# Two-layer hybrid decoder: TensorE transposes replaced by VectorE 32x32 transposes and GpSimd transfers

## The chip, the cores and the metric

One core of one Trainium2 chip runs the program. The metric is the device time of one execution in microseconds; lower is better. Times given for the kernel are medians of several executions.

## The reference, cut to what matters

The input is x of 256 tokens by 2048 features in float32. Layer one is stick-breaking attention over 16 heads of 128, layer two softmax attention with rotary embedding. With 256 tokens there is a single 256-position block, so that attention is plain causal attention.

```python
# layer one
q, k, v, z = split(x @ w_in_a, 4)          # w_in_a: 2048 x 8192
y = (stick_breaking(q, k, v) * silu(z)) @ w_out_a
x = layer_norm(alpha * x + y) * g0 + b0
x = x + (p[0] @ w_ple[0]) * sigmoid(x @ w_ple_gate[0])
# shared keys and values, then layer two
xs = layer_norm(x) * g_kv + b_kv
k, v = split(xs @ w_kv, 2); k = rope(k)
q, z = split(x @ w_in_b, 2); q = rope(q)
y = (causal_attention(q, k, v) * silu(z)) @ w_out_b
x = layer_norm(alpha * x + y) * g1 + b1
x = x + (p[1] @ w_ple[1]) * sigmoid(x @ w_ple_gate[1])
```

## The kernel before, in words

Every weight matrix is streamed once in pieces of 256 rows by 512 columns (512 KB), 388 of them and 8 halves at the start. SyncE loads them into four slots of raw. ScalarE copies a piece into w_hi in the reduced format fp32r (`split`, L417), VectorE writes the remainder raw - w_hi into w_lo (`split`, L676), and TensorE makes three products hi*hi, hi*lo, lo*hi for each half of the rows and each of two token tiles, 12 matmuls of 128x512 a piece (`piece`, L1077 to L1079). A chunk is 8 pieces: 512 output columns for all 256 tokens, in two of the four banks of acc, the next chunk in the other two. There are 8 slots of w_hi and w_lo, so the split of piece n + 8 waits until piece n is used, and it is written in the program of ScalarE and of VectorE at the place of piece n.

Around this stream everything else is an inserted step. Each engine's program is written out: in `pieces(n, base, after, before)` (ScalarE, VectorE) and `chunk(..., after)` (TensorE), `after={j: [...]}` means that the step stands behind the split, or the piece, with index j of the chunk. Engines meet through semaphores only.

- Layer one has four groups of 4 heads. Each has a q, k, v and z chunk (the order is q, k, then v, z, q of the next group, k of the next group). `evacuate` (L696) copies the finished chunk to big0, in rows by token. Matmuls of the attention need q, k and z with features on the partitions: `q_turn` behind piece 4 of the k chunk, `k_turn` behind piece 2 of the v chunk and `z_turn` behind piece 2 of the next q chunk transpose them on TensorE, eight 128x128 transposes each, into the PSUM tile aux (`transposes`, L1104; `z_turn`, L1170). ScalarE and VectorE read aux (`q_copies`, `k_copies`, `silu_z`, `queries_lo`, `keys_lo`). `key_scores`, `cumulate` and `weigh_values` are the attention's matmuls.
- The output projection of a layer is followed by one piece for each of four chunks of p @ w_ple (`ple_and_gate`), between which the normed result is transposed for the gate projection (`ln_turn`, L870 applies gain and offset, L430 and L691 split the operand), and by four gate chunks. `sigmoid_gate` and `add_ple` finish a chunk; in layer one `add_ple` leaves the sum in stage, copies it to res (L907), and `x2_turn` transposes it on TensorE for layer two. GpSimd writes the result to x2_spill.
- Layer two has four q chunks, four z chunks and four pairs of key and value chunks. `ln_step` transposes the normed layer-one result (the key/value operand), `q_turn_b` the rotated q, `z_turn_b` z, all on TensorE.
- GpSimd issues only the few transfers of p, tables, residual and spill, and copies q's first half for layer two's attention (L398).

The last gate chunk of layer two ends the stream: two sigmoids, two products, two sums and two stores follow.

## Time and profile before

| quantity | value |
|---|---|
| median of 3 runs | 1170.33 us (1170.27 to 1170.63) |
| the profiled execution's own time | 1170.72 us |
| its span in the profile | 1168.8 us |
| TensorE busy | 1161.9 us, 99% |
| VectorE busy | 740.9 us, 63% |
| ScalarE busy | 591.1 us, 51% |
| GpSimd busy | 21.3 us, 2% |
| moved by DMA | 221.49 MB, mean 189 GB/s |

In the rows, PE is TensorE, PEld its weight load, DVE VectorE, ACT ScalarE, POOL GpSimd and SP SyncE; a q behind the name is that engine's sequencer. L with a number is a line of the kernel. The DMA issues of GpSimd count as busy time of POOL in the timeline.

### The profile page before, as it was taken

To read this page: it belongs to the slowest core of one execution; us is meant where nothing else is said; L and a number is where in the kernel's file an instruction comes from. 1 tells how busy PE (TensorE), PEld (TensorE's weight loads), DVE (VectorE), ACT (ScalarE), POOL (GpSimd) and SP (SyncE) were. 2 spreads that over 40 slices of the span, in tenths; PEclk is the share of its full clock that TensorE was granted. 3 is DMA by queue.
4 is the path that set the end of the run, shared out by engine and by line. 5 is a ranking of instruction groups with operands and counts; after the bars stand their busy time and mean duration, and the time that the engine had idled before them with its cause. 6 is when DMAs were issued, how large, how long until landed. Compare 5 with 4: busy or idle time off the path is not lost.

```text
span 1168.8 us, 15615 instructions
## 1 busy us (share of the span) xinstructions
PE 1161.9 (99%) x5484; PEld 971.4 (83%) x5484; DVE 740.9 (63%) x786; ACT 591.1 (51%) x669; POOL 21.3 (2%) x43
## 2 busy tenths in 40 slices
PE   9999999999999999999999999999999999999998
PEld 7888888888888888888888888888888888888886
DVE  6765556556556556688777665446677666656863
ACT  6665465456446543455444445544555545435541
POOL 1000000000000000000000000000000000000000
PEclk9999999999999999999999999999999999999999
DMA  9855656665565776457765655655545575763671
GB/s 307 287 161 178 181 162 178 179 181 161 165 194 156 241 253 200 137 184 237 232 198 162 197 180 182 193 181 164 169 155 178 167 244 175 252 195 112 211 252 41
DMA packets 112618, 221.49 MB, mean 189 GB/s; under 512 B 6929, under 2 KB 8977, under 8 KB 112065
## 3 DMA queue, kind: packets, MB, share of 16 engines
q1 hardware_dynamic: 110032, 209.74, 57.7%
q0 software_dynamic: 2544, 11.19, 2.7%
q8 instruction: 27, 0.44, 0.1%
q14 instruction: 15, 0.11, 0.0%
HBM read 216.71 MB, written 4.19 MB: 189 GB/s over the span
## 4 chain that ended last, share of the span: by engine, by line
PE 95%; DVE 2%; DMA 1%; ACT 1%; issue 0%; SPq 0%; ACTq 0%; DVEq 0%
PE acc L1077 29%; PE acc L1079 29%; PE acc L1078 29%; PE aux L1104 2%; PE aux L1121 2%; DVE w_lo L676 1%; PE aux L1145 1%; DVE stage L870 1%; PE aux L1159 1%; DMA raw<-in_w_ple_gate 1%; PE aux L1308 0%; DMA raw<-in_w_in_a 0%; DVE act L691 0%; PE aux L1079 0%; PE aux L1078 0%
## 5 line engine op out<-in xcount | busy, mean ns | idle before, releaser
L676 DVE TENSOR_TENSOR w_lo<-raw,w_hi 128x1024 fp32r<-128x1024 f32 x388 | 471.7, 1224 | 358.5 <-ACT w_hi L417 357.2
L417 ACT ACTIVATE w_hi<-raw 128x1024 fp32r<-128x1024 f32 x388 | 409.7, 1060 | 471.3 <-PE acc L1079 424.5
L1077 PE MATMUL acc<-w_hi,act 128*128 128x512 f32 x1552 | 611.9, 394 | 0.2 <-DVE w_lo L767 0.2
L1079 PE MATMUL acc<-w_hi,act 128*128 128x512 f32 x1552 | 605.1, 390 | 0.0
L1078 PE MATMUL acc<-w_lo,act 128*128 128x512 f32 x1552 | 604.1, 389 | 0.0
L1079 PEld LDWEIGHTS acc<-w_hi,act 128*128 128x128 f32 x1552 | 291.3, 188 | 61.8
L1077 PEld LDWEIGHTS acc<-w_hi,act 128*128 128x128 f32 x1552 | 291.5, 188 | 58.6 <-issue 1.0
L1078 PEld LDWEIGHTS acc<-w_lo,act 128*128 128x128 f32 x1552 | 291.7, 188 | 58.1
L430 ACT ACTIVATE act<-stage 128x1024 fp32r<-128x1024 f32 (+1 forms) x12 | 12.7, 1061 | 33.8 <-DVE stage L870 33.8
L513 ACT ACTIVATE heads<-aux,neg_max 128x128 f32<-128x128 f32 (+1 forms) x32 | 13.0, 419 | 23.7 <-DVE neg_max L1000 23.7
L691 DVE TENSOR_TENSOR act<-stage,act 128x1024 fp32r<-128x1024 f32 (+1 forms) x12 | 14.7, 1226 | 14.3 <-ACT act L430 14.3
L870 DVE TENSOR_SCALAR stage<-aux,ln_col 128x256 f32<-128x256 f32 x48 | 22.8, 538 | 0.9 <-PE aux L1104 0.9
L1104 PEld LDWEIGHTS aux<-ident,big 128*128 128x128 f32 x128 | 14.9, 140 | 2.1
L1104 PE MATMUL aux<-ident,big 128*128 128x128 f32 x128 | 16.6, 272 | 0.0
L696 DVE TENSOR_SCALAR big<-acc 128x1024 f32<-128x1024 f32 x12 | 14.6, 1218 | 0.0
L701 DVE SCALAR_TENSOR_TENSOR heads<-aux,heads 128x768 f32<-128x768 f32 x8 | 7.6, 954 | 10.8 <-ACT heads L483 10.8
L430 ACT ACTIVATE act<-heads 128x1024 f32 (+1 forms) x8 | 8.5, 1062 | 10.4 <-DVE heads L752 10.0
L691 DVE TENSOR_TENSOR act<-heads,act 128x1024 f32 (+1 forms) x8 | 9.8, 1225 | 5.7 <-ACT act L430 5.2
L417 ACT ACT_TABLE_LOAD x9 | 11.5, 1283 | 0.2
L630 ACT ACTIVATE stage<-acc 128x512 f32<-128x512 f32 x2 | 1.2, 598 | 19.1 <-PE acc L1079 19.1
L891 DVE TENSOR_TENSOR big<-big,heads (+1 forms) x8 | 9.8, 1225 | 0.9
L943 DVE TENSOR_TENSOR stage<-stage,big 128x512 f32<-128x512 f32 x2 | 1.4, 688 | 14.0 <-ACT stage L630 14.0
(148 smaller groups left out, 617.5 us busy)
## 6 DMA issues: line engine op xcount, KB each, us to landing
raw<-in_w_in_a SPq DMA_DIRECT2D x124, 512.0 KB, 3.7
raw<-in_w_ple_gate SPq DMA_DIRECT2D x64, 512.0 KB, 4.8
raw<-in_w_in_b SPq DMA_DIRECT2D x64, 512.0 KB, 3.7
raw<-in_w_kv SPq DMA_DIRECT2D x64, 512.0 KB, 3.7
raw<-in_w_out_a SPq DMA_DIRECT2D x32, 512.0 KB, 4.4
raw<-in_w_out_b SPq DMA_DIRECT2D x32, 512.0 KB, 4.9
heads<-in_ln_rows POOLq DMA_DIRECT2D x4, 1024.0 KB, 8.2
raw<-in_w_ple SPq DMA_DIRECT2D x8, 512.0 KB, 4.6
```

The costliest lines, as they stand in the source:

```text
L417: nc.scalar.activation(w_hi[:, r], raw[:, r % RAWS], ACT.Copy).then_inc(hi_ready, 1)
L430: nc.scalar.activation(quarter(dst[:, 0], c), src, ACT.Copy).then_inc(act_hi, 1)
L513: last = nc.scalar.activation(prob[:, b, h, lo:hi], aux_b[:, 2 * b + h, lo:hi], ACT.Exp, bias=neg_max[:, b, i:i + 1], accum_out=row_sum[:, ...
L676: nc.vector.tensor_tensor(w_lo[:, r], raw[:, r % RAWS], w_hi[:, r].bitcast(F32), ALU.subtract) \
L691: nc.vector.tensor_tensor(quarter(dst[:, 1], c), src, quarter(dst[:, 0], c).bitcast(F32), ALU.subtract).then_inc(act_ready, 1)
L696: nc.vector.tensor_scalar(dst, acc_of(parity), 1.0, None, ALU.mult).then_inc(chunk_evac, 1)
L870: last = nc.vector.tensor_scalar(stage_kt[:, i], aux_kt[pair][:, i], g, b, ALU.mult, ALU.add)
L1077: nc.tensor.matmul(dst, hi, w_hi[:, r, i], start=begin, stop=False)
L1078: nc.tensor.matmul(dst, hi, w_lo[:, r, i], start=False, stop=False)
L1079: mm = nc.tensor.matmul(dst, lo, w_hi[:, r, i], start=False, stop=end)
L1104: mm = nc.tensor.transpose(dst[:, i, t * P:(t + 1) * P], src[:, t, i * P:(i + 1) * P], ident[:, :])
L1121: mm = nc.tensor.matmul(dst, lhs(a), rhs(b), start=start and i == 0, stop=True, skip_group_check=True)
```

## The change

Twenty-seven times a group of eight TensorE transposes is taken out: q, k and z of layer one, three of the four chunks of its result, the key/value operand, and q and z of layer two. In its place VectorE transposes each 32x32 block of the 128x1024 data within its quadrant (`turn_squares` reads the finished chunk from PSUM and stands where the evacuation stood; `turn_queries`, `turn_normed` and a line of `add_ple` read SBUF). Then GpSimd issues 16 transfers (`exchange`), each from 32 partitions by 256 elements to 32 other partitions, which put the blocks into their places. The users read the result from SBUF with an order of blocks (`by_square`). k_copies, q_copies and the rest of layer one's attention stand two pieces later, weigh_values stands behind pieces 0 and 1 of the following chunk. Of the transposes on TensorE remain those of the gate operands, the last chunk of layer one's result, and k of layer two.

Besides, the fourth w_ple piece of layer two moves to the end of the stream (`last_ple_product`), with a copy of p's parts (`keep_p`), and the last products and sums are made in three parts. Layer one's `add_ple` writes the sum straight to res.

```diff
+            def exchange(turned, count, dst, src, moved):
+
+                pool.wait_ge(turned, count)
+                for a in range(NS):
+                    for g in range(NS):
+                        pool.dma_start(dst[g * SQUARE:(g + 1) * SQUARE, a * HT // NS:(a + 1) * HT // NS],
+                                       src[a * SQUARE:(a + 1) * SQUARE, g * HT // NS:(g + 1) * HT // NS]) \
+                            .then_inc(moved, 16)
+
+            for g in range(G):
+                exchange(chunk_evac, g * 4 + 1, qT_flat, qn, q_moved)
+                exchange(chunk_evac, g * 4 + 2, kT_flat, kn, k_moved)
+                exchange(chunk_evac, g * 4 + 4, gt_flat, zn, z_moved)
             pool.wait_ge(pv_done, 2 * G)
             load_res(0, x)
...
+            for c in range(G):
+                if c < G - 1:
+                    exchange(x2_turned, c + 1, stage[:, :], vz_flat, x2_moved)
                 pool.wait_ge(x2_ready, c + 1)
...
+            for c in range(G):
+                exchange(ln_turned, c + 1, gt_flat, stage[:, :], ln_moved)
+                exchange(q_turned, c + 1, qT_flat, kT_flat, q_moved)
+            for c in range(G):
+                pool.wait_ge(sz_ready, c + G)
+                exchange(chunk_evac, c + (C_Z + 1), gt_flat, vz_flat, z_moved)
...
             def k_copies(k):
 
-                act.wait_ge(kT_psum, k + 1)
-                nc.scalar.activation(kT[:, :, P:T], aux_kt[1][:, :, P:T], ACT.Copy).then_inc(kT_ready, 1)
-                nc.scalar.activation(k_parts[:, 0], aux_kt[1][:, :, 0:P], ACT.Copy).then_inc(k_hi, 1)
+                act.wait_ge(k_moved, k * MOVED + MOVED)
+                nc.scalar.activation(by_square(k_own), kT_x[:, 1::TT], ACT.Copy).then_inc(kT_ready, 1)
+                nc.scalar.activation(by_square(k_parts[:, 0]), kT_x[:, 0::TT], ACT.Copy).then_inc(k_hi, 1)
...
             def after_k(k):
-                return {4: [lambda: q_copies(k)]}
+                return {5: [lambda: q_copies(k)]}
 
             def after_v(k):
-                return {2: [lambda: k_copies(k)], 4: [lambda: exp_abs(k, 0)],
-                        5: [lambda: exp_abs(k, 1), lambda: log_1p(k)],
-                        6: [lambda: softplus_hi(k, 0)], 7: [lambda: softplus_hi(k, 1), lambda: values_hi(k)]}
+                return {4: [lambda: k_copies(k)], 6: [lambda: exp_abs(k, 0)],
+                        7: [lambda: values_hi(k), lambda: exp_abs(k, 1), lambda: log_1p(k)]}
...
-            def evacuate(n_end, parity, dst):
+            def turn_squares(n_end, parity, dst):
+
                 dve.wait_ge(piece_used, n_end)
-                nc.vector.tensor_scalar(dst, acc_of(parity), 1.0, None, ALU.mult).then_inc(chunk_evac, 1)
+                nc.vector.transpose(turned_squares(dst), turned_rows(acc_of(parity))).then_inc(chunk_evac, 1)
...
             def v_steps(k, n):
-                return {2: [lambda: keys_lo(k)], 5: [lambda: softplus(k, 0)], 6: [lambda: softplus(k, 1)],
-                        7: [lambda: softplus_lo(k, 0), lambda: values_lo(k), lambda: evacuate_v(n, 0, vn_a)]}
+                return {5: [lambda: keys_lo(k)],
+                        7: [lambda: values_lo(k), lambda: evacuate_v(n, 0, vn_a), lambda: softplus(k, 0)]}
...
-            def after_v(k, c):
-                return {2: [lambda: k_turn(k, c - 1)], 4: [lambda: key_scores(k, 0)],
-                        5: [lambda: key_scores(k, 1)]}
+            def after_v(k):
+                return {6: [lambda: key_scores(k, 0)],
+                        7: [lambda: key_scores(k, 1)]}
...
+            def last_ple_product():
+
+                r = N_LAST % SPLITS
+                pe.wait_ge(lo_ready, N_LAST + 1)
+                pe.wait_ge(p_kept, 1)
+                for bank, (t, lo, hi) in enumerate(LAST_PARTS):
+                    for i in range(PIECE_K):
...
+                    mm.then_inc(last_ple, 1)
```

In the order of VectorE's program the v chunk of layer one starts, before, with the splits of pieces 0 to 4 (w_lo) and the low part of the keys (k_parts) behind the third:

```order
L676 TENSOR_TENSOR w_lo<-raw,w_hi 128x1024 [waits act_hi_ready]
L675 REGISTER_ALU
L676 TENSOR_TENSOR w_lo<-raw,w_hi 128x1024 [waits act_hi_ready]
L675 REGISTER_ALU
L676 TENSOR_TENSOR w_lo<-raw,w_hi 128x1024 [waits act_hi_ready]
L728 REGISTER_ALU
L729 TENSOR_TENSOR k_parts<-aux,k_parts 128x512 [waits act_k_hi]
L675 REGISTER_ALU
L676 TENSOR_TENSOR w_lo<-raw,w_hi 128x1024 [waits act_hi_ready]
```

Of the change, the same chunk from the fourth split on:

```order
L746 TENSOR_TENSOR w_lo<-raw,w_hi 128x1024 [waits act_hi_ready]
L745 REGISTER_ALU
L746 TENSOR_TENSOR w_lo<-raw,w_hi 128x1024 [waits act_hi_ready]
L745 REGISTER_ALU
L746 TENSOR_TENSOR w_lo<-raw,w_hi 128x1024 [waits act_hi_ready]
L799 REGISTER_ALU
L800 TENSOR_TENSOR k_parts<-heads,k_parts 128x512 [waits act_k_hi]
L745 REGISTER_ALU
L746 TENSOR_TENSOR w_lo<-raw,w_hi 128x1024 [waits act_hi_ready]
```

The keys' low part now stands behind the sixth split (index 5) and reads heads, where the transfers put k, in place of aux.

GpSimd's program between the constants and the output projection of layer one, before (p, tables, then the residual x):

```order
L366 DMA stage<-in_pt 128x2x256 [waits pe_piece_used,act_masks_done,dve_operand_ready]
L383 DMA cos_sin<-in_rope 128x256
L384 DMA ln_col<-in_ln_cols 128x96
L361 DMA big<-in_x 128x2x512 [waits pe_pv_done]
L361 DMA big<-in_x 128x2x512 x3
```

And of the change, the end of the same stretch (q, k and z of the fourth group, then the residual):

```order
L430 DMA heads<-big 32x256 [waits dve_chunk_evac]
L430 DMA heads<-big 32x256 x15
L430 DMA heads<-big 32x256 [waits dve_chunk_evac]
L430 DMA heads<-big 32x256 x15
L430 DMA heads<-big 32x256 [waits dve_chunk_evac]
L430 DMA heads<-big 32x256 x15
L400 DMA big<-in_x 128x2x512 [waits pe_pv_done]
L400 DMA big<-in_x 128x2x512 x3
```

Twelve exchanges of 16 transfers now stand ahead of the residual's four on GpSimd.

## Rows read from the trace of the kernel before

**Rows 1.** The page, parts 1 and 2: busy us of each engine, and TensorE's clock.
```profile
PE 1161.9 (99%) x5484; PEld 971.4 (83%) x5484; DVE 740.9 (63%) x786; ACT 591.1 (51%) x669; POOL 21.3 (2%) x43
...
PEclk9999999999999999999999999999999999999999
```

**Rows 2.** Waits of TensorE: us in total, times, longest.
```profile
PE aux L1104 <- DVE big L907: 0.2, 1, 0.2
```

**Rows 3.** The chain in order of time: start us, us, what; layer two's q and z chunks.
```profile
642.21 0.87 PE aux L1104 x8
...
665.79 0.87 PE aux L1104 x8
...
734.71 0.87 PE aux L1104 x8
757.37 0.87 PE aux L1104 x8
```

**Rows 4.** Timeline 146 to 172 (start, us, engine): k chunk's end, second v chunk.
```profile
148.89 1.06 ACT L417 ACTIVATE w_hi<-raw 128x1024 fp32r<-128x1024 f32 x1 [1.94 <-PE acc L1079]
...
151.12 1.22 DVE L696 TENSOR_SCALAR big<-acc 128x1024 f32<-128x1024 f32 x1
...
156.51 1.03 PE L1104 MATMUL aux<-ident,big 128*128 128x128 f32 x8
156.71 1.06 ACT L417 ACTIVATE w_hi<-raw 128x1024 fp32r<-128x1024 f32 x1 [1.66 <-PE acc L1079]
157.68 0.58 ACT L446 ACTIVATE heads<-aux 128x512 f32<-128x512 f32 x1
157.80 1.23 DVE L676 TENSOR_TENSOR w_lo<-raw,w_hi 128x1024 fp32r<-128x1024 f32 x1 [1.50 <-ACT w_hi L417]
158.15 0.59 ACT L447 ACTIVATE k_parts<-aux 128x512 fp32r<-128x512 f32 x1
158.95 0.69 DVE L729 TENSOR_TENSOR k_parts<-aux,k_parts 128x512 fp32r<-128x512 f32 x1
```

**Rows 5.** Timeline of GpSimd (x4: four issues in a row), then VectorE beside it.
```profile
25.08 0.54 POOL L384 DMA_DIRECT2D ln_col<-in_ln_cols  x1
394.43 2.88 POOL L361 DMA_DIRECT2D big<-in_x  x4 [368.81 <-PE aux L1159]
409.84 1.10 POOL L370 DMA_DIRECT2D heads<-in_ln_rows  x2 [12.54 <-DVE act L691]
...
394.16 1.23 DVE L676 TENSOR_TENSOR w_lo<-raw,w_hi 128x1024 fp32r<-128x1024 f32 x1 [2.71 <-ACT w_hi L417]
395.30 1.22 DVE L696 TENSOR_SCALAR big<-acc 128x1024 f32<-128x1024 f32 x1
```

**Rows 6.** DMA view: queues with packets, MB, share; issues with KB, us to landing.
```profile
q1 hardware_dynamic: 110032, 209.74, 57.7%
q0 software_dynamic: 2544, 11.19, 2.7%
...
x_spill<-big POOLq DMA_DIRECT2D x4, 512.0 KB, 3.2
...
cos_sin<-in_rope POOLq DMA_DIRECT2D x1, 128.0 KB, 4.6
```

**Rows 7.** Timeline 1062 to 1110: the first gate matmul and the operand's last quarter.
```profile
1075.56 0.47 PE L1077 MATMUL acc<-w_hi,act 128*128 128x512 f32 x1
...
1090.51 1.23 DVE L691 TENSOR_TENSOR act<-stage,act 128x1024 fp32r<-128x1024 f32 x1 [1.13 <-ACT act L430]
```

**Rows 8.** Timeline 1155 to 1169: the last matmul, sigmoid, product and sum.
```profile
1163.39 0.39 PE L1079 MATMUL acc<-w_hi,act 128*128 128x512 f32 x1
...
1163.82 0.60 ACT L630 ACTIVATE stage<-acc 128x512 f32<-128x512 f32 x1 [0.76 <-PE acc L1079]
...
1164.53 0.68 DVE L943 TENSOR_TENSOR stage<-stage,big 128x512 f32<-128x512 f32 x1
...
1165.24 0.69 DVE L946 TENSOR_TENSOR big<-big,stage 128x512 f32<-128x512 f32 x1
```

**Rows 9.** Groups by line: busy us, mean ns of one, idle before.
```profile
L706 DVE TENSOR_TENSOR heads<-heads,past 128x256 f32<-128x256 f32 x16 | 6.1, 422 | 0.3
...
L907 DVE TENSOR_SCALAR big<-stage 128x1024 f32 (+1 forms) x4 | 2.8, 694 | 0.1
```

More of the change, by code:

```diff
@@ L319, in load_out_ple_gate @@
                     load(n + i, (n + i) % SPLITS, w_out, j, c)
-                for c in range(G):
+                for c in range(G - layer):
                     load(N_PLE[layer] + c, (N_PLE[layer] + c) % SPLITS, w_ple[layer], 0, c)
@@ L615, in out_ple_gate @@
                                        [lambda c=c: full_hi(k + c, c) for c in range(G)])
[L617 to L620 removed]
+                turns = {0: ple_step[0:1] + [lambda r=r: normalise(2 * layer, r, r) for r in x1]
+                         + ple_step[1:2] + full_step[0:1] + ple_step[2:3] + full_step[1:2] + ple_step[3:G - layer]}
+                turns |= {1: full_step[2:3], 2: [keep_p]} if layer else {2: full_step[2:3]}
+                pieces(n, n, count=G - layer, before=turns)
                 n = N_GATE[layer]
@@ L869, in full_quarter, with gate_quarter @@
                         g, b = (ln_col[:, which, s, bass.ds(c * HG + i, 1)] for s in range(2))
-                    last = nc.vector.tensor_scalar(stage_kt[:, i], aux_kt[pair][:, i], g, b, ALU.mult, ALU.add)
+                    dst, part = (stage_kt[:, i], src[:, i]) if which < LAYERS else \
+                        (by_square(stage_kt[:, i:i + 1]), src[:, TT * i:TT * (i + 1)])
+                    last = nc.vector.tensor_scalar(dst, part, g, b, ALU.mult, ALU.add)
                 last.then_inc(full_ready, 1)
+            def gate_quarter(k, c, layer, s):
+                dve.wait_ge(lnT_psum, k + 1)
+                dve.wait_ge(act_ready, s)
+                full_quarter(c, aux_kt[c % 2], layer)
             def full_lo(s, c):
@@ L931, in out_ple_gate @@
                        before={0: turned[3]})
-                with dve.Fori(1, G - layer) as c:
-                    pieces(c * PC + n, n, ({3: [lambda: x2_lo(c - 1)]} if layer == 0 else {})
-                           | {5: [lambda: gain_and_offset(layer, c)], PC - 1: [lambda: add_ple(layer, c)]})
+                if layer == 0:
+                    for c in range(1, G):
+                        pieces(c * PC + n, n, {5: [lambda: gain_and_offset(0, c)], 6: [lambda: x2_lo(c - 1)],
+                                               PC - 1: [lambda: add_ple(0, c, c < G - 1)]})
+                else:
+                    with dve.Fori(1, G - 1) as c:
+                        pieces(c * PC + n, n, {5: [lambda: gain_and_offset(1, c)], PC - 1: [lambda: add_ple(1, c)]})
@@ L935, in out_ple_gate @@
                 if layer:
                     c = G - 1
+                    pieces(n + c * PC, n, count=1)
                     gain_and_offset(layer, c)
-                    dve.wait_ge(ple_evac, 2 * G)
                     dve.wait_ge(x1_ready, 2 * G)
-                    for t in range(TT):
-                        r, gate = columns(res[1], c)[:, t], stage_tn[:, t]
+                    for i, (t, lo, hi) in enumerate(LAST_PARTS):
+                        r, gate = columns(res[1], c)[:, t, lo:hi], stage_tn[:, t, lo:hi]
@@ L990, in k_end @@
+            pieces(N_Z, N_Z, {2: [lambda: ln_quarter(G - 1)], 3: [lambda: ln_lo(G - 1)]} | z_end(0, 0))
+            for c in range(1, G):
+                pieces(c * PC + N_Z, N_Z, z_end(c, c % 2))
             def k_end(n, g):
@@ L1194, in _ @@
             chunk(0, 0, act0, 0, 0, quarters=S_X)
-            chunk(PC, 0, act0, 1, 1, after=after_k(0, 1))
+            chunk(PC, 0, act0, 1, 1)
             pe.wait_ge(masks_done, 1)
@@ L1210, in ln_turn @@
                 pe.wait_ge(normed_1, k + 1)
[L1211 removed]
+                transposes(columns(src, c), aux_kt[pair], lnT_psum)
             def out_projection(layer, after_out):
@@ L1236, in ple_and_gate @@
                 pe.wait_ge(p_ready, layer + 1)
-                for c in range(G):
+                for c in range(G - layer):
                     n = N_PLE[layer] + c
@@ L1248, in ple_and_gate @@
                 chunk(n, n, act0, 0, c0, quarters=s, after={1: [lambda: turn(3)]})
-                pe.wait_ge(ple_evac, layer * G + G)
+                if layer == 0:
+                    pe.wait_ge(ple_evac, G)
                 with pe.Fori(1, G - layer) as c:
-                    chunk(c * PC + n, n, act0, c % 2, c + c0,
-                          after={3: [lambda: x2_turn(c - 1)]} if layer == 0 else None)
+                    chunk(c * PC + n, n, act0, c % 2, c + c0)
                 if layer:
```

313 lines of the change are left out of this document (164 added, 149 removed).

## The prediction

> **What bounds the kernel now.** I read the page's busy shares first: TensorE is busy 1161.9 of 1168.8 us at full granted clock [rows 1]. Then its waits: one of 0.2 us after the start, and nothing else of weight [rows 2]. So every microsecond taken out of TensorE's stream is a microsecond of the span, as long as nothing else grows into a wait. The chain in order of time shows what a transpose group costs there: eight 128x128 transposes stand as one piece of 0.87 us [rows 3]. The spacing is the better price: with two groups a chunk lasts 665.79 - 642.21 = 23.58 us, with one 757.37 - 734.71 = 22.66 us, so a group is worth 0.92 us, a chunk without one 21.74 us, and one piece of eight 2.72 us.
>
> Below, T is the end of a chunk on TensorE and T + 2.72 j the end of the next chunk's j-th piece. Every weight piece is split by ScalarE and VectorE eight pieces ahead of its use, but only once the piece eight earlier is used; [rows 4] shows the rhythm: ScalarE starts 0.1 us after a piece's end, VectorE 1.09 us later.
>
> **The change part by part.**
>
> 1. Groups taken from TensorE. Layer one's q, k and z: 3 x 4; its result: 3 of 4; layer two's key/value operand, q and z: 3 x 4. That is 27 groups of eight: 27 x 0.92 = **-24.8 us**. By the 0.87 us piece it would be 23.5.
>
> 2. What replaces them, per group: one VectorE block transpose of 128x1024, where in 16 of the 27 a plain evacuation goes (1.22 us, [rows 4]), then 16 transfers of 32 KB issued by GpSimd, then reads from SBUF. The trace has no such transpose. The nearest row is the evacuation, same elements, same PSUM source: I take 1.22 us and 2.4 as the upper bound (half rate). VectorE is 63% busy on the page [rows 1], and its work is off the path while the split stays ahead; the 11 additional transposes cost nothing then. Without cover each would cost its 1.2 us, 13 in all. The GpSimd issue: four DMAs of 256 rows took 2.88 us (0.72 each), two of 128 rows 1.10 (0.55), one of 48 KB and 128 rows 0.54 [rows 5]. The new ones have 32 rows each. From 256 to 128 rows the price falls by 0.17 to 0.18; the same slope (1.35 ns a row) to 32 rows gives 0.42, an estimate from these rows. I take 0.45, 7.2 us for sixteen, bounds 0.42 and 0.72. Landing: the spill lands 3.2 us after its issue, the upper bound is 4.6 [rows 6]; I take 3.5 after the last issue.
>
> 3. Which use comes due first. q is turned at the end of its chunk and used by ScalarE after piece 5 of the next: T + 6 x 2.72 + 1.2 = T + 17.5. z and the layer-one result are due at T + 17.5 and T + 20.2, layer two's q at T + 20.2, its LN operand in the next chunk. Only **k** is tight. Its transpose follows the split on VectorE and ends at T + 3.6 (in [rows 4] the evacuation ends at 152.34, 3.55 after the piece's end). Landed: T + 3.6 + 7.2 + 3.5 = T + 14.3. ScalarE's copies stand behind the split of piece 4, T + 5 x 2.72 + 1.2 = T + 14.8. So k is there, with 0.5 us in hand, about 0.9 before it holds the next split. The queues: in layer one GpSimd has three exchanges in four chunks; in a layer-two q chunk it has two, 32 issues or 14.4 us of 21.7.
>
> 4. A wait that the new order adds even with k on time. VectorE's keys_lo now stands behind the split of piece 5, and TensorE wants the scores after piece 6. From [rows 4]: split start on ScalarE 156.71, keys_lo ends 158.95 + 0.69 = 159.64, 2.93 later. The next piece ends 2.72 - 0.1 = 2.62 after that split start. TensorE waits 0.3 us, four times: **+1.3 us**. In the old order two pieces lay between. The other attention steps keep two pieces or more: cumulate is due at about T + 15.6 of the z chunk (the first scores' 2 us and five pieces) against a softplus low part at about T + 13.
>
> 5. Layer two's last w_ple piece leaves the stretch between output projection and gate. TensorE reaches the gate's pieces 2.72 us earlier, while VectorE and ScalarE still make the gate's operand. The last quarter is needed at piece 6: before, 1092.9 (start 1075.56, six pieces, one group), and it was ready at 1090.51 + 1.23 = 1091.74 [rows 7], 1.2 early. Now it is needed at 1090.2 on that clock; one weight split less (1.22) stands ahead of it on VectorE but ScalarE gets a copy of p (1.06), so it is ready near 1091.0. **+0.9 us**; bounds 0 and 2.7.
>
> 6. The end. The piece reappears as 18 matmuls behind the last gate chunk and covers the sigmoids. Before, the last matmul ends at 1163.78 and the last add at 1165.93, 2.15 later [rows 8]. Now the first bank is ready 1.36 us into the 2.72 us of the piece; two operations of 0.69 and four on 256 elements (0.42 each, [rows 9]) follow, one behind the other: 1.36 + 1.38 + 1.68 = 4.4, plus semaphores 4.5, or 1.8 after TensorE's end. **-0.4 us**, the last transfer being half the size included.
>
> 7. At no cost: layer one's gate chunks lose a plain copy of the sum (0.69, [rows 9]) and gain a transpose. The residual copy through GpSimd for x moves behind z's exchange, due 38 us (14 pieces) into the output projection. The qT copy of GpSimd moves behind all exchanges, due in the second key/value chunk.
>
> Sum against the profiled execution, 1170.72 us: -24.8 + 1.3 + 0.9 - 0.4 = -23.0, so 1147.7; the median of the runs lies 0.4 below that execution: **1147.3 us**.
>
> **Two rules weighed.** At [rows 5] four issues took 0.72 us each while VectorE ran a two-input SBUF subtraction from 394.16 to 395.39 and an evacuation after it; the two other issues of 0.55 match one made alone (0.54). Nothing of a block is to be seen.
> The Trainium skill speaks against this change here: SBUF — State Buffer, section "A bandwidth-pool intuition that's wrong", says that GpSimd cannot write descriptors while VectorE holds the port that both share, and gives 620 ns growing to about 3100 ns under a VectorE copy. That is rival B; for the subtraction, [rows 5] do not agree.
> At [rows 3] a 128x128 f32 transpose costs TensorE 0.87/8 = 0.109 us in a row of eight. VectorE: DVE Perf Modes, section "The three transpose paths", gives 390 ns for one on TensorE; by that figure the 27 groups would be 84 us (an estimate from that page). The trace's own duration is used.
>
> **Rivals.**
>
> A, k lands late. ScalarE blocks in k_copies, and behind it queue the split of piece 5 (1.1), VectorE's split (1.2) and keys_lo (0.7), with the copies (1.2) some 4.1 us in all. With i per issue and L to land, TensorE waits 3.6 + 16 i + L + 4.1 - 19.0 = 16 i + L - 11.3 per group, once that is over 0.3. At i = 0.55 and L = 4.6 it is 2.1, four times 8.4: 1154.4. At i = 0.72 and L = 3.5 it is 3.7, 15 us, and 32 issues take 23.0 us of a 21.7 us q chunk, 4 us more: 1165. For it: 0.54 is the cheapest issue that the trace has. Against: all of those have four times the rows. Chance 0.22.
>
> B, VectorE's subtractions hold GpSimd up. An exchange of 7.2 us meets 2.6 splits of 1.22 us, +3.2: 7.2 + 3.2 + 3.5 - 11.3 = 2.6 per group, 10.4 in place of 1.3: 1156.4. Chance 0.04.
>
> C, GpSimd becomes the bound and the kernel slower. The place is the layer-two q chunks, with two exchanges each, beside the k wait. At 1 us per issue (no row shows it, but none shows a transfer from SBUF to SBUF with both ends cut in 32 rows either): k costs 4 x 8.2 = 33 us, the q chunks last 32 in place of 21.7 us, three and a half times: 36. With the 24.8 gained, about +44: 1215. It decides from 0.76 us per issue. Against: nothing in [rows 5] is over 0.72 with eight times the rows. Chance 0.05.
>
> D, the transfers starve the weights. A weight packet costs 57.7% of 16 x 1168.8 us by 110032, 98 ns [rows 6]; a chunk's 2048 packets take 12.5 of its 21.7 us. An exchange has 512 packets of 1 KB: 3.1 us at that price, two per chunk 6.3, which fits in 9.2 idle. At the GpSimd queue's 198 ns per packet (2.7%, 2544) they take 12.7, 3.5 too many in four chunks: 14 us, 1161. Those packets are four times as large. Chance 0.03.
>
> **How the numbers follow.** Forecast 0.66; A 0.22, B 0.04, C 0.05, D 0.03. The forecast's own ends: no wait of steps 4 and 5 at all, 1145; both at twice the size, 1149.5. To hold 8 in 10 the range reaches into A as far as i near 0.6: 1145 to 1156. No change is what lies within 0.2% (2.3 us), about what a measurement can tell. Faster: all but C and a thin edge of A, 0.94; same 0.01; slower 0.05.
>
> **What would show it.** Right: the transposes' group gone from 27 places, chunks without one at 21.7 us; GpSimd issues near 0.45 us, sixteen in a row; the block transpose near 1.2 us; TensorE waiting for keys_lo four times by 0.3 us and once by about 1 us at the last gate's start; ScalarE's k copies starting right behind their split. Wrong: waits for k of over 1 us, with ScalarE idle on the GpSimd transfers (A, B); GpSimd without a pause in layer two (C); ScalarE idle on the weights in those chunks (D); a block transpose far over 2.4 us, which would eat VectorE's lead.

## The result, and the profile after

The changed kernel takes **1161.82 us** (median of four runs, 1158.9 to 1163.39) against 1170.48 us before in the same comparison: a ratio of 0.9919, 95% interval 0.9907 to 0.9932. It is faster by 8.7 us, where 23 were forecast; the time lies 5.8 us above the upper end of the range. The profiled execution took 1162.06 us with a span (first to last instruction) of 1160.3 us.

From the page of the changed kernel, parts 1 to 3 [rows 1, rows 6]:

```profile
PE 1142.2 (98%) x5274; PEld 952.9 (82%) x5274; DVE 746.6 (64%) x795; ACT 591.0 (51%) x669; POOL 233.3 (20%) x475
...
PEclk9989999999999999999999999999999999999999
...
q0 software_dynamic: 16368, 25.37, 6.8%
```

TensorE's stream did get shorter, 1161.9 to 1142.2 us, but 18 us of the span are now idle where 7 were, and one slice of the clock's line is down. The waits of TensorE (total, times, longest) say where [rows 2]:

```profile
PE aux L1218 <- DVE k_parts L800: 9.6, 4, 8.4
PE aux L1211 <- DVE big L980: 3.1, 1, 3.1
```

Of the first, 8.4 us are one wait, in the first group of heads; the other three are 0.4 us each. The second is the end of layer one's gate.

A kernel that loses time in a few places is best read by the times at which it reaches the same points of its work. These are rows of the chain in order of time, first before, then after; L1145 and L1244 are the first cumulative sum of a group of heads of layer one (after: of the first two groups), L1104 and L1211 transposes that stay on TensorE: the first of layer one's norm, the last of layer one's result, and the first k of layer two. Two more of this pattern are used and not shown: the fourth group's first cumulative sum, called the fourth cumulate below (375.77 before, 383.31 after), and the first transpose of layer two's norm (1067.67 and 1059.62).

```profile
84.76 1.09 PE aux L1145 x8
...
487.59 0.89 PE aux L1104 x8
...
595.01 0.87 PE aux L1104 x8
...
802.71 0.87 PE aux L1104 x8
```

```profile
98.56 1.09 PE aux L1244 x8
...
193.46 1.09 PE aux L1244 x8
...
488.77 0.89 PE aux L1211 x8
...
596.10 1.38 PE aux L1211 x8
...
794.66 0.87 PE aux L1211 x8
```

The differences make a table of stretches, each a difference of two such rows (the last one: to the end of the span). "Forecast" is the row of before plus the prediction's terms that fall into the stretch; in the first it also has two pieces (5.44 us) more, because attention comes two pieces later, and in the third those two pieces less.

| stretch, us | before | forecast | after | e4 | e5 | e8 | e9 |
|---|---|---|---|---|---|---|---|
| A: start to the first cumulate | 84.76 | 88.7 | 98.56 | 89.28 | 96.33 | 88.78 | 88.23 |
| B: to the fourth cumulate | 291.01 | 283.6 | 284.75 | 282.84 | 284.72 | 284.71 | 282.84 |
| C: to layer one's norm | 111.82 | 105.5 | 105.46 | 105.46 | 105.45 | 105.46 | 105.46 |
| D: to the last turn of its result | 107.42 | 104.7 | 107.33 | 107.03 | 104.28 | 106.77 | 107.45 |
| E: to layer two's first k | 207.70 | 196.7 | 198.56 | 196.73 | 196.76 | 196.96 | 196.98 |
| F: to its norm | 264.96 | 265.0 | 264.96 | 264.96 | 264.96 | 264.96 | 264.93 |
| G: to the end | 101.13 | 101.6 | 100.68 | 100.80 | 100.70 | 100.76 | 100.71 |

C, F and G came out as forecast or a little better. The error is 9.9 us in A, 1.2 in B, 2.6 in D, 1.9 in E, less 0.9 in G: 14.7 by these rounded figures, and the profiled execution is 14.4 us above the 1147.7 forecast for it. Each column is one profiled execution; A and D differ from one execution to the next, as e3 and e10 will show.

**Stretch A.** The chain from k's block transpose on (start us, us, what):

```profile
59.56 1.26 DVE big L767
...
61.09 7.34 POOL heads L430 x15
68.43 5.52 DMA heads<-big
```

And the timeline beside it, with each engine's idle time in brackets:

```profile
38.69 1.25 DVE L767 STREAM_TRANSPOSE big<-acc 128x1024 f32<-128x1024 f32 x1
...
40.23 7.87 POOL L430 DMA_DIRECT2D heads<-big  x16 [15.00 <-DVE big L767]
...
53.16 1.06 ACT L501 ACTIVATE big<-heads 128x1024 f32<-128x1024 f32 x1 [3.98 <-DMA heads<-big]
...
56.14 1.23 DVE L746 TENSOR_TENSOR w_lo<-raw,w_hi 128x1024 fp32r<-128x1024 f32 x1 [5.71 <-ACT w_hi L478]
...
73.97 0.63 ACT L507 ACTIVATE big<-heads 128x512 f32<-128x512 f32 x1 [6.21 <-DMA heads<-big]
```

Two exchanges are late one behind the other. The sixteen issues of q take 7.87 us and its last transfer lands at 53.1. ScalarE, in its program's order, stands in front of the q copy for 3.98 us and makes no splits; VectorE runs dry for 5.71 us; so k's block transpose starts only at 59.56. Then k's own sixteen issues follow and a landing of 5.5 us, counted from the start of the last issue; ScalarE stands still for another 6.21 us, and TensorE for 8.4. The block transpose itself takes 1.25 us against the 1.22 of the prediction.

And q was late before its exchange began. TensorE's stream starts, before and after, with

```profile
6.11 0.48 PE L1077 MATMUL acc<-w_hi,act 128*128 128x512 f32 x1
```

```profile
6.83 0.48 PE L1184 MATMUL acc<-w_hi,act 128*128 128x512 f32 x1
```

Eight pieces of 2.72 us later, near 28.6 in the changed kernel, the q chunk is finished, but VectorE turns it only at 38.69, 10 us later: the transpose stands behind a split whose weights land at 36.4. The kernel before shows the same in its evacuation, near 11 us behind the end of its chunk, where it cost nothing:

```profile
38.94 1.22 DVE L696 TENSOR_SCALAR big<-acc 128x1024 f32<-128x1024 f32 x1
```

After the wait TensorE's granted clock is down (columns: PE, PEld, DVE, ACT, POOL busy, PEclk, DMA share, GB/s):

```profile
61.00:74.00 13.00, 8.67 (x39) 6.84 (x37) 5.63 (x5) 3.22 (x4) 7.84 (x16) 1.00 0.90 280
74.00:82.00 8.00, 3.93 (x16) 3.63 (x17) 2.96 (x3) 4.40 (x6) 0.00 (x0) 0.57 0.35 99
```

0.57 is a stretch mostly at the lower of the two levels, 1.2 GHz instead of 2.4. From the first scores to the first cumulate it takes 20.5 us here and 19.0 in e4 and e8, where the clock stays up: 1.5 us. With the 8.1 us by which the wait exceeds the forecast 0.3, that is nearly all of A's 9.9.

**The exchanges** as a whole, in the view of the line that issues them (duration ns minimum/median/maximum; first and last start):

```profile
L430 POOL DMA_DIRECT2D heads<-big x192: 498/498/522, 40.2 to 405.1; - x192
...
DMA to landing us min/median/max: 1.7/3.5/6.8
```

An issue costs 498 ns, not 450. The median landing of a single transfer is the 3.5 us that was taken for the last one; the last transfers of the first exchanges take 5.5 and one of layer one's result 6.8.

**Stretch D.** One turn of the chain through layer one's gate:

```profile
534.31 6.75 DMA raw<-in_w_ple_gate
541.16 1.07 ACT w_hi L478
...
546.93 1.23 DVE act L989
...
549.39 1.24 DVE stage L977
550.65 1.24 DVE big L980
551.91 1.25 DVE v_or_z L984
...
554.32 2.27 DVE w_lo L746 x2
556.74 6.61 DMA raw<-in_w_ple_gate
...
583.11 6.78 DMA stage<-v_or_z
```

TensorE isn't in this turn. The loop runs from a weight's landing through ScalarE's split, VectorE's row of elementwise work with the new block transpose (L984), to the split that frees a raw buffer, and so to the next weight's transfer. It takes 556.74 - 534.31 = 22.43 us, more than the 21.74 us that TensorE now needs for a chunk and less than the 22.66 it needed with one group. The last row is the end of the third exchange: in the last chunk ScalarE waits 2.9 us for it, in front of the last sigmoid, so the chain leaves the loop there. ScalarE's waits for these weights between 505 and 597 us rose to 24.2 us, with 5.3 as the longest (before: 10.2 and 2.7):

```profile
ACT w_hi L478 <- DMA raw<-in_w_ple_gate: 24.2, 15, 5.3
```

### The profile page after: what moved, and what is told of

It reads as the page before. It is cut to its first block, busy times and chain, and to the rows that moved or that the text cites. A ratio compares the mean times of both kernels' runs of the same rounds, so it can differ in the third digit from the quotient of the medians.

```text
span 1160.3 us, 15528 instructions
## 1 busy us (share of the span) xinstructions
PE 1142.2 (98%) x5274; PEld 952.9 (82%) x5274; DVE 746.6 (64%) x795; ACT 591.0 (51%) x669; POOL 233.3 (20%) x475
## 3 DMA queue, kind: packets, MB, share of 16 engines
q0 software_dynamic: 16368, 25.37, 6.8%
## 4 chain that ended last, share of the span: by engine, by line
PE 83%; DVE 6%; DMA 5%; ACT 2%; POOL 2%; issue 1%; SPq 0%; ACTq 0%; DVEq 0%
PE acc L1184 26%; PE acc L1186 25%; PE acc L1185 25%; PE aux L1218 2%; DMA raw<-in_w_in_a 2%; DVE w_lo L746 2%; DMA raw<-in_w_ple_gate 2%; POOL heads L430 1%; ACT w_hi L478 1%; DMA heads<-big 1%; PE aux L1211 1%; PE aux L1244 1%; DVE stage L942 1%; POOL stage L430 1%; PE aux L1258 1%
## 5 line engine op out<-in xcount | busy, mean ns | idle before, releaser
L430 POOL DMA_DIRECT2D heads<-big x192 | 94.1, 498 | 286.2 <-DVE big L767 242.5
L430 POOL DMA_DIRECT2D heads<-v_or_z x64 | 31.3, 498 | 51.9 <-DVE v_or_z L767 39.0
L430 POOL DMA_DIRECT2D stage<-v_or_z x48 | 23.6, 501 | 71.4 <-DVE v_or_z L984 70.3
L430 POOL DMA_DIRECT2D heads<-stage x64 | 31.5, 499 | 18.1 <-DVE stage L1072 16.6
L430 POOL DMA_DIRECT2D heads<-heads x64 | 32.1, 510 | 8.6 <-DVE heads L1060 8.4
L491 ACT ACTIVATE act<-stage 128x1024 fp32r<-128x1024 f32 (+1 forms) x12 | 12.7, 1061 | 32.4 <-DVE stage L942 32.4
L761 DVE TENSOR_TENSOR act<-stage,act 128x1024 fp32r<-128x1024 f32 (+1 forms) x12 | 14.7, 1223 | 9.0 <-ACT act L491 9.0
L1218 PE MATMUL aux<-q_parts,k_parts 128*128 128x256 f32 x48 | 9.9, 322 | 9.6 <-DVE k_parts L800 9.6
L1218 PEld LDWEIGHTS aux<-q_parts,k_parts 128*128 128x128 f32 x48 | 7.6, 206 | 11.5 <-issue 11.2
L942 DVE TENSOR_SCALAR stage<-aux,ln_col 128x256 f32<-128x256 f32 x32 | 15.2, 538 | 0.9 <-PE aux L1211 0.9
L767 DVE STREAM_TRANSPOSE big<-acc 128x1024 f32<-128x1024 f32 x12 | 14.9, 1244 | 0.0
```

The source lines that it names most:

```text
L430: pool.dma_start(dst[g * SQUARE:(g + 1) * SQUARE, a * HT // NS:(a + 1) * HT // NS], src[a * SQUARE:(a + 1) * SQUARE, g * HT // NS:(g + 1) ...
L491: nc.scalar.activation(quarter(dst[:, 0], c), src, ACT.Copy).then_inc(act_hi, 1)
L761: nc.vector.tensor_tensor(quarter(dst[:, 1], c), src, quarter(dst[:, 0], c).bitcast(F32), ALU.subtract).then_inc(act_ready, 1)
L767: nc.vector.transpose(turned_squares(dst), turned_rows(acc_of(parity))).then_inc(chunk_evac, 1)
L942: last = nc.vector.tensor_scalar(dst, part, g, b, ALU.mult, ALU.add)
L1218: mm = nc.tensor.matmul(dst, lhs(a), rhs(b), start=start and i == 0, stop=True, skip_group_check=True)
```

## The experiments

e1 to e10 are runs; the changed kernel is the base of each unless said otherwise. Theory: q and k of the first group, and layer one's result, arrive late, and that is all that is missing. Rivals on the cause of the lateness: the order in which ScalarE and VectorE stand in front of it, the sixteen issues, or the load of the transfers on the DMA engines. All times of before in these comparisons are 1170.89 to 1171.14 us.

**e1: q later in the first chunk of k.** ScalarE's q copies and VectorE's work on q go from behind the sixth piece to behind the eighth; k's block transpose no longer stands behind q.

```diff
-            pieces(PC, 0, after_k(0))
+            pieces(PC, 0, {7: [lambda: q_copies(0)]})
...
-            pieces(PC, 0, k_steps(0, PC))
+            pieces(PC, 0, {7: [lambda: turn_squares(2 * PC, 1, kn), lambda: queries_lo(0)]})
```

> Edit: in the first k chunk alone, ScalarE's q copies stand behind the split of piece 7 in place of 5, and VectorE turns k before it makes q's low part. Theory 1 (a late q holds the queue): the 8.4 us wait of TensorE in the first group comes from ScalarE's 4.0 us wait for q, which holds up the splits and so the turning of k, which ends at 60.8. Without it k is turned near 54.5, sixteen issues of 0.49 and a landing of 5.5 us bring it at 68, and TensorE waits 16 x 0.49 + 5.5 - 11.3 = 2 us: some 6.4 us of wait and 1 to 2 us of slow clock less, 1154. Theory 2 (the busy DMA queues at the start are enough by themselves): q's place does not matter, the wait stays over 6 us, 1160 or more.

Measured: 1154.98 us (1154.33 to 1157.91), ratio 0.986 (0.9844 to 0.9877). In its profile k's issues begin at 57.10 instead of 61.09, the longest wait for k is 4.2 instead of 8.4 us, and A is 94.43 instead of 98.56. Nothing else in the table moves. So the late q did cost, through the two queues, some 4 us by the profiles and 6.8 by the medians; 5.7 us of A's loss remain, and the wait is twice the 2 us expected. In this profile the chain to k's block transpose (55.57) no longer holds the q copy but a transfer of weights of 7.76 us.

**e2: layer one's result back on TensorE.** The three exchanges of stretch D are undone, and with them their block transposes.

```diff
-                    exchange(x2_turned, c + 1, stage[:, :], vz_flat, x2_moved)
...
+            def x2_turn(c):
+                pe.wait_ge(x2_ready, c + 1)
+                pe.wait_ge(act_ready, c + S_X2)
+                transposes(columns(res[0], c), aux_kt[0], x2T_psum)
```

> Edit: the three chunks of layer one's result are transposed on TensorE again (and read from PSUM behind piece 3); all else as changed. Theory 1 (the transfers cost more than they save there): the 3.1 us wait at 596 us and the slow clock behind it, 4.6 us by matched times, go; three groups of 0.92 come back: 1161.8 - 4.6 + 2.8 = 1160. ScalarE's waits for gate weights fall from 35.8 towards 20 us. Theory 2 (the gate weights run late without the transfers too): the wait stays, 1164.6.

Measured: 1159.9 us (1159.45 to 1160.65), ratio 0.9906 (0.989 to 0.9923). The wait of 3.1 us is gone, D is 107.02 and E 196.74. Taking these three groups off TensorE had gained 0 in D (107.33 with them off, 107.02 with them on) and cost 1.8 us in E through the lower clock. By these stretches the three of 27 groups were a loss of 2 us. The medians differ by 1.9 us too, but the intervals of the two ratios overlap.

**e3: both.**

> The edits of the q copies' place and of layer one's result together. Theory 1: the gains add, 1152. Theory 2: one of them only moves the wait to the other place, 1158 or more.

Measured: 1154.46 us (1152.3 to 1157.47), ratio 0.9851 (0.9835 to 0.9868); longest wait for k 4.9 us, A 95.76, D 107.03, E 196.73. By the medians e2's edit adds only 0.5 us to e1's; by the profiles its 2.2 us in D and E are there, and A happened to be 1.3 longer than e1's. A differs from one execution to the next, with this part of the program unchanged.

**e4: both, and the keys' low part one split earlier.** VectorE's keys_lo stands behind the split of piece 4 in every group.

```diff
-                return {5: [lambda: keys_lo(k)],
+                return {4: [lambda: keys_lo(k)],
```

> Both edits, and keys_lo behind the split of piece 4 in place of 5 on VectorE. If the wait for the keys' low part is that of the program order, the three later groups lose their 0.65 us each (0.4 of wait and what the restart costs), and the first group's path is shorter by the two splits, 2.2 us: 1148. If k's landing alone sets the time, nothing changes against the two edits, 1152.

Measured: **1149.23 us** (1148.2 to 1150.35), ratio 0.9814 (0.9797 to 0.983): the fastest kernel of the study that leaves nothing out, 12.6 us under the changed one and some 22 under the kernel before. From TensorE's waits, and from its chain:

```profile
PE aux L1213 <- DVE k_parts L798: 0.7, 1, 0.7
```

```profile
89.28 1.09 PE aux L1239 x8
...
183.56 1.09 PE aux L1239 x8
```

The spacing of the cumulates falls from 94.9 to 94.28 us. So the wait of 0.4 us, with what follows it, was worth 0.64 us a group; the prediction had 0.3. In the first group the order counts too: from k's landing to the first scores it is 4.12 us in the changed kernel, e1 and e3, and 2.04 in e4. The other 4.4 us of A's 6.5 between e3 and e4 are k landing 1.9 us earlier in this execution, and the clock, which stays up behind a wait of 0.7 (2.5 us).

**e5: a quarter of the bytes.** Sixteen issues of 32 rows as before, with 256 bytes a row.

```diff
-                        pool.dma_start(dst[g * SQUARE:(g + 1) * SQUARE, a * HT // NS:(a + 1) * HT // NS],
-                                       src[a * SQUARE:(a + 1) * SQUARE, g * HT // NS:(g + 1) * HT // NS]) \
+                        pool.dma_start(dst[g * SQUARE:(g + 1) * SQUARE, a * HT // NS:a * HT // NS + 64],
+                                       src[a * SQUARE:(a + 1) * SQUARE, g * HT // NS:g * HT // NS + 64]) \
```

> Edit on the changed kernel: every transfer of an exchange carries 64 of its 256 elements a row, so as many transfers, issues and packets, and a quarter of the bytes (heads is set to zero once at the start). It leaves out three quarters of the moved data, so what follows is computed from wrong values. Theory 1 (the bytes load the DMA queues, and that makes the landings and the weights late): the last landing of the first two exchanges falls from 5.5 towards 3.5 us, TensorE's wait at the first scores from 8.4 to 3 to 5 us, the wait at 596 us is gone, and ScalarE's waits for gate weights fall from 35.8 towards 20 us; 1152 to 1155. Theory 2 (the number of packets and issues, or the weight stream by itself, sets them): landings, waits and time stay, 1160 to 1163.

Measured: 1155.15 us (1154.65 to 1157.26), ratio 0.987 (0.9855 to 0.9885). Its chain in A and its milestone at the end of D:

```profile
47.55 4.31 DMA heads<-big
...
67.16 3.48 DMA heads<-big
...
590.78 0.87 PE aux L1214 x8
```

The issues still take 498 ns. The landings shorten from 5.5 to 4.3 and 3.5 us and k lands 3.3 us earlier, of which 2.2 us reach A; 5.4 us of wait for k are left, just above the 3 to 5 expected. D becomes 104.28: the whole gain forecast there, with no wait and no drop of the clock. ScalarE's waits for gate weights did not fall, as Theory 1 had it, but are 39.0 us against 35.8 over the whole run. The drop of 6.7 us between the medians is more than A's 2.2, so D and E gained in more than the profiled execution, and bytes are the likely cause in D; e10 will show a D of 105.0 with all the bytes, so this one column does not prove it. In A they are the smaller part.

**e6: the last w_ple piece of layer two back in its old place**, on top of e4, with the last chunk's end in two parts.

```diff
-    N_GATE[1] = N_PLE[1] + G - 1
-    N_LAST = N_GATE[1] + G * PC
+    N_GATE[1] = N_PLE[1] + G
...
-        LAST_PARTS = ((0, 0, COLS), (1, 0, COLS // 2), (1, COLS // 2, COLS))
+        LAST_PARTS = ((0, 0, COLS), (1, 0, COLS))
```

> Edit on e4: the fourth w_ple piece of layer two stands between output projection and gate again, and the end has its two parts. If the terms of the prediction hold (0.9 us lost at the gate's start, 0.4 won at the end), this is 0.5 us faster than e4, 1148.7. If the matched times of the two profiles hold (0.45 us won by that part of the change), it is 0.4 to 0.5 slower, 1149.7.

Measured: 1151.97 us (1150.15 to 1152.34), ratio 0.9834 (0.9821 to 0.9848), against 1149.23 for e4. The sign is that of the second expectation. In the profiles G is 1149.4 - 1047.64 = 101.76 against 100.80; the rest of the difference is A again, 90.61 against 89.28. But up to the last sum the two take 98.27 and 98.37 us. The 1.0 us lies behind it, where the last store ends: 3.5 us in e6, 2.4 in e4, and 2.9 in the kernel before, which ends in the same way as e6. So the move of that piece gains 0.5 to 1.0 us, through the smaller last store and not through TensorE's stream.

**e7: each exchange in 32 issues of half rows.** The same bytes in twice the issues.

```diff
+                        for b in range(2):
+                            to, at = a * HT // NS + b * HT // NS // 2, g * HT // NS + b * HT // NS // 2
+                            pool.dma_start(dst[g * SQUARE:(g + 1) * SQUARE, to:to + HT // NS // 2],
+                                           src[a * SQUARE:(a + 1) * SQUARE, at:at + HT // NS // 2]) \
```

> Edit on the changed kernel: every transfer is made as two of half the row (128 elements), so 32 issues an exchange. Theory 1 (GpSimd's price is per issue, 0.49 us whatever the bytes): an exchange takes 15.7 us to issue; TensorE waits 15.7 + 3.5 - 11.3 = 8 us in each of four groups, and a q chunk of layer two lasts 31.4 us in place of 21.7; about 1162 + 4 x 7 + 3.5 x 9.7 = 1220 less what hides, slower than the kernel before. Theory 2 (the price goes with the bytes or rows moved): 0.25 us per issue, and nothing changes, 1162.

Measured: 1288.55 us in its one run, 117 us slower than the kernel before. From its page (busy; the chain's shares by engine), and below it TensorE's waits:

```profile
PE 1164.8 (91%) x5274; PEld 965.9 (75%) x5274; DVE 743.0 (58%) x795; ACT 586.3 (46%) x669; POOL 444.4 (35%) x907
...
PE 47%; POOL 30%; DVE 7%; DMA 6%; issue 5%; ACT 4%; SPq 0%; ACTq 0%; DVEq 0%; POOLq 0%
```

```profile
PE aux L1220 <- DVE k_parts L802: 59.2, 4, 16.1
PE acc L1186 <- DVE w_lo L748: 28.7, 11, 4.7
PE acc L1186 <- ACT big L559: 14.4, 1, 14.4
PE aux L1213 <- DVE big L982: 14.0, 1, 14.0
```

A half row costs an issue the same 498 ns, so the exchange takes 15.9 us, and the issues' number rules the time. GpSimd is 35% busy and yet makes up 30% of the chain: its place between two engines counts, not its busy share. The four rows sum to 116 us of waits against 12.7 in the changed kernel, and TensorE's stream itself is 22.6 us longer at a mean granted clock of 0.955 (0.995 in the changed kernel); 103.6 + 22.6 is nearly all of the 126.5 us between the two spans. This is rival C's case (1 us for what one issue did), which the prediction priced at 1215, and it is some 68 us above the run's own expectation, in which an exchange did not make the next one late.

**e8: four issues of 128 rows.** The same bytes in the same packets of 1 KB, but a quarter of the issues; the permutation between squares is what this leaves out.

```diff
-                    for g in range(NS):
-                        pool.dma_start(dst[g * SQUARE:(g + 1) * SQUARE, a * HT // NS:(a + 1) * HT // NS],
-                                       src[a * SQUARE:(a + 1) * SQUARE, g * HT // NS:(g + 1) * HT // NS]) \
+                    pool.dma_start(dst[:, a * HT // NS:(a + 1) * HT // NS],
+                                   src[:, a * HT // NS:(a + 1) * HT // NS]) \
```

> The changed kernel with each exchange issued as 4 transfers of 128 rows of 1 KB instead of 16 of 32 rows. The bytes and the packets are the same; what is left out is the permutation between the squares (rows stay on their partitions, so the matrices are only transposed within blocks). Theory 1 (the time of GpSimd's sixteen issues of 498 ns is what makes q and k of the first group and the gate operand of layer one late): four issues at 0.54 to 0.55 us take 2.2 us, an exchange ends 5.7 us earlier, the waits for q, for k (all but the 0.4 us of keys_lo) and of 3.1 us at the gate go: 10.2 - 0.7 at the start, 2.7 + 1.9 around the gate: 1162 - 14 = 1148, at most 1151. Rival (the transfers wait in the DMA engines behind the weights, so that issuing them sooner only lengthens the landing): the first k lands as late as the e5 run's at best, 70.6 us, with a landing of 8 us or more behind the last issue, and the time stays at 1155 or above.

Measured: 1152.4 us (1150.19 to 1153.32), ratio 0.9844 (0.9827 to 0.986); the profiled execution took 1150.19. The issuing line's view, then TensorE's waits, then milestones of the chain:

```profile
L429 POOL DMA_DIRECT2D heads<-big x48: 537/537/539, 40.0 to 389.5; - x48
```

```profile
PE aux L1210 <- DVE big L979: 2.5, 1, 2.5
PE aux L1217 <- DVE k_parts L799: 1.6, 4, 0.4
```

```profile
88.78 1.09 PE aux L1243 x8
...
585.72 1.09 PE aux L1210 x8
```

A is 88.78 us, the forecast's 88.7: with 2.15 us per exchange instead of 7.9, no q and no k is late, at the same bytes and behind the same weights. The rival fell for A. In D I had expected the wait to go too, and it did not: 106.77 us, a wait of 2.5, and the same loop as above in the chain, 546.84 - 524.68 = 22.16 us a turn. The exchanges of D land in 2.1 us (median) and are no longer in the chain, so here it is neither the issues nor the rival's longer landing, but the loop itself. Sooner issues don't help it. The expected 1148 was missed by the 2.1 us of D in the profiled execution; the median lies 1.4 us above the 1151 that were to be the most.

**e9: e8 with the keys' low part behind piece 4.**

> e8 with the keys' low part of layer one behind the split of piece 4 instead of piece 5 (as in e4). Leaves out the same permutation. Theory 1: the four waits of 0.4 us and their restarts (0.66 each) go as well, now in all four groups: e8 minus 2.5 us, 1145 to 1147. Rival (k's copies on ScalarE are not there yet at piece 4 and the low part holds VectorE's next split): same as e8 or slower.

Measured: 1149.54 us (1148.4 to 1150.08), ratio 0.9818 (0.9802 to 0.9835). No wait for k is left, A is 88.23 and B 282.84 (94.28 a group). D is 107.45, with a wait of 3.2 us, and that is why the time stays above the 1147 expected.

**e10: the keys' low part alone**, all sixteen issues kept.

> The changed kernel with only the keys' low part behind the split of piece 4, sixteen issues kept, nothing left out. If the order on VectorE is the cause of the 0.4 us waits in groups 2 to 4, the spacing of the cumulates falls from 94.9 to 94.3 us, and the time by about 2 us, to 1160; the first group (k landed at 73.95 in the changed kernel) keeps its loss. Rival (k's copies are themselves late there, by the 0.34 us that ScalarE waits): no gain, 1162.

Measured: 1158.06 us (1152.97 to 1159.76), ratio 0.9895 (0.9878 to 0.9911), 3.8 below the changed kernel. The profile fell on the fastest execution. Its spacing, 189.62 - 95.34 = 94.28 us, settles the point on the order:

```profile
95.34 1.09 PE aux L1244 x8
...
189.62 1.09 PE aux L1244 x8
```

In B that is 1.9 us. The first group gains by the order as well, which the expectation had ruled out: from k's landing (72.92) to the first scores it is 2.04 us instead of 4.12. Together 4.0, for the 3.8 between the medians, whose ratios' intervals just overlap. The runs of this kernel lie up to 6.8 us apart. In the profiled one D was 105.0 us, with a wait of 0.7 only, at a program that is unchanged there. So both A and D vary from one execution to the next; what decides it stays open.

## Why the prediction was wrong

**The bound** was right. TensorE's stream was the span, and it gave up 19.7 us of busy time; the lower clock, which lengthened it again, took most of the rest of the 23.5 that 27 pieces of 0.87 us make.

**Step 1** (27 groups x 0.92) holds where nothing waits: C fell by 6.36 us, the one group and two pieces; E by 10.94 to 10.97 in e4 and e5 for twelve groups, 11.04 forecast.

**Step 2** mis-sized the issue. "From 256 to 128 rows the price falls by 0.17 to 0.18; the same slope (1.35 ns a row) to 32 rows gives 0.42" ran a line through two points on to a third; measured are 0.72 at 256 rows [rows 5], 0.537 at 128 and 0.498 at 32. Below 128 rows almost nothing is left to save, and bytes change nothing (e5, e7). An exchange's issues take 7.87 us for the 7.2 taken. The landing of 3.5 us is right as a median, but the upper bound of 4.6 was read off one single transfer [rows 6], and here it is the last of sixteen that counts: 5.5 us in the first group, 6.8 in the gate.

**Step 3** is the step that failed. Its due times start from "q is turned at the end of its chunk", and it concludes "Only **k** is tight". In the first group VectorE turned q not at T + 0 but 10 us behind the chunk's end, because in its program the transpose stands behind a split that was waiting for weights; the trace of before had that delay, at 38.94 us. With 13.2 us of issues and landing for 10.7, q landed at 53.1, T + 24.5, where it was due at T + 17.5. ScalarE, itself late by its own waits for weights (0.2 to 1.6 us before each split from 39 us on), stood in front of the q copy from 49.18 on. What then counted was not that TensorE needs q but that ScalarE's queue stops there, and k's block transpose behind that: it ended 6.9 us behind its T + 3.6, k's own exchange took 2.4 us more than forecast, and k landed 9.3 us late. The prediction followed such a queue for k, in rival A, and not for q. The parts do not add up to shares: with exchanges of four issues (e8) q and k are both in time in spite of the late start, with q out of the queue (e1) some 4 us come back, with a quarter of the bytes (e5) 2.2 us. No run takes away the late start of q itself; that part is read from the traces.

**Step 3 again, and step 7**: layer one's result was put down as due at T + 20.2, and its changes in the gate chunks as "At no cost". Taking one group from each of three chunks left TensorE 21.74 us a chunk and made a loop of VectorE and the weights' transfers the longest one, 22.43 us a turn. The extra 1.25 us block transposes stand in that loop, and "the 11 additional transposes cost nothing then" was read off VectorE's average of 63%. e2, which puts the three groups back, ends the wait at the same D; e8 shows the loop without the late exchange. **Rival D** had the right kind of cause, transfers beside weights, but looked for it in layer two's q chunks, where E shows nothing (196.73 to 196.98 with the exchanges; the 1.9 us of the changed kernel's E are the clock), and counted packets against idle time instead of asking whose landing a loop waits for.

**Step 4** was right in place and kind and low in size: 0.4 us for 0.3 in the waits, 0.64 with the restart, four times; e4, e9 and e10 show that one place earlier in VectorE's order removes it.

**The clock** was not priced. After the waits of 8.4 and 3.1 us TensorE ran at the lower level for a while: A lost 1.5 us by it, and the eight transposes behind the second wait took 1.38 instead of 0.87 us, and E lost 1.9.

**Steps 5 and 6** came to -0.45 us in G for +0.5 forecast. No wait for the gate's operand stands in TensorE's waits, so step 5's 0.9 was too much: up to the last sum G is 98.39 us, 0.13 more than before. The gain lies behind that sum, 2.3 us for 2.9, in a last store of half the size. The end is as step 6 has it, a chain of small operations, 1.7 us behind TensorE's end (1.8 forecast, 2.15 before):

```profile
1155.00 0.69 DVE L1031 TENSOR_TENSOR stage<-aux,stage 128x512 f32<-128x512 f32 x1 [14.91 <-PE aux L1354]
...
1157.58 0.43 DVE L1033 TENSOR_TENSOR big<-big,stage 128x256 f32<-128x256 f32 x1
```

From the first product to the last sum it is 3.01 us for the 3.06 of the prediction's durations. The prediction's 1092.9 for the operand's due time should be 1092.8 by its own terms; nothing hangs on it.

**Rival A** is what happened, but in one group and by 8 us instead of in four by 2; its formula had k's own issues and landing and not the delays in front of k's transpose. In groups two to four ScalarE waits some 0.4 us for k, (7.4 - 6.2) / 3, and TensorE's 0.4 is step 4's. **Rival B** fell: 192 issues of q, k and z last 498 ns and at most 522, those between 61.1 and 68.9 us too, beside VectorE's splits. The Trainium skill, in SBUF — State Buffer, section "A bandwidth-pool intuition that's wrong", gives the block of GpSimd's descriptor writing for a VectorE tensor_copy. The fp32 subtractions here do not cause one, so the prediction was right to give that price little weight; no run here was made to test a copy. **Rival C** was real: e7 is its case, and at 1288 its price had been far too low, because a late exchange makes the next one late (B grew by 49 us, E by 57) and the waits lower the clock. The measured issue, 0.50 us, lies 0.26 us below the 0.76 from which this rival was to decide.

## What to carry to other kernels

When work moves from the bounding engine to a path of several engines and transfers, its due time must be found for every queue it stands in, at the start and at each phase's own rhythm, from the trace's times of before (here the evacuation at 38.94) and not from the steady rhythm, and not only for the engine that uses it last: each in-order engine that stops in front of it passes the delay to everything behind. Count issues, not bytes, for GpSimd's own time, and bytes for the landing; and before taking more out of a stream, work out the period of the next loop (buffer freed, transfer, split, freed again), since a gain beyond it is not paid out and a wait there can cost clock as well. If an exchange can't be made cheaper, look for single steps to move: two entries in an order table (e1, e4) and giving up the three groups that gained nothing were worth 12.6 us here, more than the change itself.

## What the runs showed of the hardware

- A GpSimd DMA issue from SBUF to SBUF lasts 498 ns for 32 rows of 1 KB (changed kernel), 512 bytes (e7) or 256 bytes (e5) alike, 537 ns for 128 rows of 1 KB (e8); the issues of 256 rows from DRAM took 720 [rows 5].
- The q0 queue's 16368 packets took 6.8% of 16 x 1160.3 us, 77 ns each, and a quarter of their bytes 4.1%. From issue to landing a transfer of an exchange took 3.5 us in the median, 1.7 to 6.8.
- A VectorE 32x32 block transpose of 128x1024 fp32 from PSUM takes 1.24 to 1.25 us, nearly the same as the evacuation of that size (1.22).
- TensorE's granted clock was 0.57 in the 8 us behind a wait of 8.4 us, and the lower level was seen behind a wait of 3.1 us too (one matmul every 0.43 us instead of every 0.23). What it cost did not follow the wait's length: behind waits of 8.4, 7.2, 5.4, 5.2, 4.9 and 4.2 us (changed kernel, e2, e5, e10, e3, e1) the way from the first scores to the first cumulate was 1.5, 2.1, 2.6, 1.4, 2.5 and 1.6 us above the 19.0 of e4. In e8 and e9 waits of 2.5 and 3.2 us at the end of D left the clock at 1.00 (584 to 600 us in both). What sets these apart from the 3.1 us stays open.
